# The ends of two hybrid layers, and their fifth unit: the splits of the third and fourth layer in another order on ScalarE and VectorE

## The chip, the cores and the metric

The kernel runs on one core of one Trainium2 chip. The metric is the device time in microseconds. Engine names are those of the profile: PE is TensorE, DVE is VectorE, ACT is ScalarE, POOL is GpSimd, SP is SyncE, which here issues every DMA.

## What is computed

Four layers run one after another on a stream x of 512 positions by 1024 channels, in float32. The first two (a gated spatial and pooling mixer, and latent attention with 16 heads) are not touched. The last two are one and the same hybrid layer with different weights:

```
def hybrid_layer(x, c_act, norm_g, w_ada, b_ada, w_in, w_out, pos):
    shift, scale, gate = jnp.split(c_act @ w_ada + b_ada, 3, axis=-1)
    h = rms_norm_2(x, norm_g) * (1.0 + scale[:, None, :]) + shift[:, None, :]
    rq, rk, rv, rg, sq, sk, sv, sg = jnp.split(h @ w_in, split_at, axis=-1)
    y_ret = retention(rotary(rq), rotary(rk), rv)        # 4 heads of 128
    y_ret = merge_heads(y_ret) * jax.nn.silu(rg)
    y_sb = stick_breaking(sq, sk, sv)                    # 8 heads of 64
    y_sb = merge_heads(y_sb) * jax.nn.silu(sg)
    y = jnp.concatenate([y_ret, y_sb], axis=-1) @ w_out
    return x + gate[:, None, :] * y
```

Retention multiplies the scores of each head by a decay, multiplies them with the values, and normalises the result over the 128 channels of the head. Stick-breaking attention takes sigmoids of the scores and a running product over the keys.

## The kernel before

Every large matmul is done in three passes on values that are split in a high and a low part: `mm3` issues high times low (L832 to L834 in some order of operands), low times high and high times high. The high part is a rounding copy (ACT or POOL), the low part is the difference of the value and its high part (DVE). Weights come in tiles of 128 by 2048 through two buffers that alternate (and some spare ones). For each tile T, SP transfers `w_raw` once the low part of tile T-2 is done (L797), ACT writes `w_hi` (`split_tile`, L1341), DVE writes `w_lo` (L1622). SP also transfers one piece of the modulation weights with each tile, `ada_raw` (L804), behind a wait that the piece two before it has been summed by DVE (`ada_piece`, L1655 and L1663).

All engines walk the same list, `plan_steps`, and each does its own part of every step, in the list's order. So the list is the order of the queue of each engine. An operation "tile" stands at the start of each tile T: PE waits for the low part of T; ACT makes the high part of T+1, DVE its low part, and then DVE sums the ada piece that goes with T, unless the step says `late_ada`.

A hybrid layer has eight units, u = 0 to 7. Units 0 to 3 are pairs of stick-breaking heads (`SP_PAIRS` is 4), units 4 to 7 retention heads. Each has five chunks of projection: AQ and AK (first tile), AV and AG (second tile), and VT, which turns the values over. AQ, AK, AV and AG are 24 matmuls of 512 columns each. The attention of the unit before (a = u-1) is put between them: `att_scores` ahead of AQ, `att_mid` behind AV, `att_out` behind AG (only for stick-breaking pairs: it ends in the two writes of `mixf` at L2170 and L2171). For a retention unit `att_scores` is 12 matmuls on PE, then on DVE four products with the decay (L2150), on ACT three high parts (L1591), on DVE three low parts (L2156); `att_mid` is 12 matmuls on PE and a square on ACT (L1611); then come `stat_cols` (column sums on PE L1201, a mean on DVE L1848, a root on ACT L1447, a reciprocal on DVE), `stat_bcast` (four transposes, L1210) and `ret_norm` (L2178, L2179), which writes `mixf`. `att_scores` of unit 4 waits on PE until `mixf` of unit 3 is written.

The chunks AQ, AK and VT have work behind them ("post"). For a retention unit ACT copies the bank to `tmp` (L1417), DVE applies the rotation to AQ and AK (L1670 to L1674), POOL makes the high part (L2202), DVE the low part (L1788, or L1791 for VT). A bank takes its next chunk once the one before is copied out.

`mix_split` makes the high part (ACT, L1598, into `h_hi`) and the low part (DVE, L2185, into `h_lo`) of the mixed heads, in the order of MIX_ORDER, whose places 0 to 3 are the stick-breaking units and 4 to 7 the retention units 4 to 7. The output projection then starts with `out_part(i)`: six matmuls for place i into the banks of the first two output chunks, spread among the attention of the last unit. After them each output chunk is 24 matmuls, and DVE adds it to x (L1768). The end of a layer, from VT of the last unit on, reads in the list: six places of `mix_split`, VT, `stat_cols` of unit 6, `att_scores` of unit 7, `out_part` 0 to 3, `stat_bcast` and `ret_norm` of unit 6, `mix_split` of place 6, the tile step of the first output tile (with the split of the second), `att_mid` of unit 7, `out_part(4)`, `stat_cols`, `out_part(5)`, `stat_bcast`, `ret_norm`, `out_part(6)`, `mix_split` of place 7 with the ada piece on DVE, a `redux` (16 small matmuls, L968), `out_part(7)`, and the output chunks.

Of the kernel before, what the change touches and what calls it, by code (L numbers as in the profile page):

```python
# [40 lines left out]
SP_PAIRS = 4  # L41
# [3 lines left out]
SEC = 8  # L45
# [34 lines left out]
def plan_steps():  # L80

    steps = []
# [3 lines left out]
    redux_chunk = {}  # L86
    spare_tiles = []

    def begin(late_ada=False):

        T = st["T"]
        st["T"] += 1
        steps.append(dict(op="tile", T=T, late_ada=late_ada))
        return T

    def chunk(kind, T, tmp=True, post=True, cast=False, val=False, **kw):
# [88 lines left out]
    T = begin()  # L185
# [41 lines left out]
    for l in (2, 3):  # L227
# [11 lines left out]
        for u in range(8):  # L239
            a = u - 1  # L240
            T = begin()
            if u == 0:
                spare_tiles.append(begin())
            if a >= 0:
                steps.append(dict(op="att_scores", l=l, u=a, g=base + a))
            for sub, kind in enumerate(("AQ", "AK")):
                chunk(kind, T, l=l, u=u, g=base + u, sub=sub, tmp=u >= SP_PAIRS, cast=u >= SP_PAIRS,
                      val=u >= SP_PAIRS)
                if sub == 0 and 0 <= a < SP_PAIRS:
                    steps.append(dict(op="att_scores2", l=l, u=a, g=base + a))  # L250
                if sub == (u < SP_PAIRS) and 0 <= a < SP_PAIRS:
                    steps.append(dict(op="att_scores3", l=l, u=a, g=base + a))
                if sub == 0 and norm:
                    steps.append(dict(op="stat_bcast", **norm))
                    steps.append(dict(op="ret_norm", l=l, u=a - 1, s=norm["stat"]))
                    norm = None
            after_tile(T)
            T = begin() if u > 0 else spare_tiles[-1]
            chunk("AV", T, l=l, u=u, g=base + u, sub=0, tmp=False, post=False)
            if a >= 0:  # L260
                steps.append(dict(op="att_mid", l=l, u=a, g=base + a))
            chunk("AG", T, l=l, u=u, g=base + u, sub=1, tmp=False, post=False)
            if a >= 0:
                steps.append(dict(op="att_out", l=l, u=a, g=base + a))
            if u == 7:
                steps.append(dict(op="mix_split", l=l, part=range(6)))
            chunk("VT", None, l=l, u=u, g=base + u, tmp=u >= SP_PAIRS, cast=u >= SP_PAIRS)
            after_tile(T)
            if a >= SP_PAIRS:
                norm = stat(P, 1, False, "ret2", 7, (7,))  # L270

        out_tile = st["T"]
        C = st["C"] + 1

        def out_part(*part):
            steps.append(dict(op="out_part", l=l, T=out_tile, C=C, part=part))

        steps.append(dict(op="att_scores", l=l, u=7, g=base + 7))
        out_part(0, 1, 2, 3)
        steps.append(dict(op="stat_bcast", **norm))  # L280
        steps.append(dict(op="ret_norm", l=l, u=6, s=norm["stat"]))
        steps.append(dict(op="mix_split", l=l, part=(6,)))
        T = begin(late_ada=True)
        steps.append(dict(op="att_mid", l=l, u=7, g=base + 7))
        out_part(4)
        norm = stat(P, 1, False, "ret2", 7, (7,))
# [1 line left out]
        steps.append(dict(op="stat_bcast", **norm))  # L288
        steps.append(dict(op="ret_norm", l=l, u=7, s=norm["stat"]))
        out_part(6)  # L290
        steps.append(dict(op="mix_split", l=l, part=(7,)))
        redux((8, 9) if l == 2 else (11,), aside=True)
        out_part(7)
        for i in range(4):
# [11 lines left out]
def build(nc, wt, adat, colst, matst, rmatst, xt, pos, wst, bst, poolt, decayt, rot, out):  # L306
# [11 lines left out]
    with ExitStack() as ctx:  # L318
# [1008 lines left out]
        def _(act):  # L1327
# [102 lines left out]
            for d in steps:  # L1430
# [161 lines left out]
                elif op == "mix_split":  # L1592
                    l = d["l"]
                    act.wait_ge(chunk_full, AG_CHUNK[8 * (l - 2) + 7] + 1)
                    for i in d["part"]:
                        k = MIX_ORDER[i]
                        act.wait_ge(mixf_done, 8 * (l - 2) + i + 1)
                        act.activation(h_hi[:, k, :], mixf[:, k, :], ACT.Copy).then_inc(m_hi_done, 1)  # L1598
# [16 lines left out]
        def _(dve):  # L1615
# [341 lines left out]
            for d in steps:  # L1957
                op = d["op"]
                if op == "tile":
                    T = d["T"]  # L1960
                    for t in split_with(T):
                        split_tile(t)
                    if not d["late_ada"]:
                        ada_piece(T + 2 * SEC)
                elif op == "chunk":
                    if d["kind"] == "XB" and d["n"] == 0:
# [4 lines left out]
                            dve.memset(padded[:, i, 0:PAD], 0.0).then_inc(pad_done, 1)  # L1971
                        dve.wait_ge(pad_done, 4)
                    chunk(d)
                elif op == "spatial_rows":
                    dve.wait_ge(rows_full, 1)
                    for i in range(DC):
# [202 lines left out]
                    dve.tensor_tensor(mixf[:, k, :], mixf[:, k, :], bank[:, 7, :], ALU.mult).then_inc(mixf_done, 1)  # L2179
                elif op == "mix_split":  # L2180
                    l = d["l"]
                    for i in d["part"]:
                        k = MIX_ORDER[i]
                        dve.wait_ge(m_hi_done, DC * (l - 2) + i + 1)
                        dve.tensor_tensor(h_lo[:, k, :], mixf[:, k, :], f(h_hi[:, k, :]),  # L2185
                                          ALU.subtract).then_inc(m_lo_done, 1)
                    if d["part"] == (7,):
                        ada_piece(T + 2 * SEC)
                elif op == "final":
                    dve.wait_ge(stb_done, d["s"] + 1)  # L2190
                    for n in range(DC):
                        dve.scalar_tensor_tensor(outf[:, n, :], x[:, n, :], col("final_g", n), bank[:, 6, :],  # L2192
                                                 ALU.mult, ALU.mult).then_inc(fin_done, 1)
# [219 lines left out]
```

## Time and profile before

| | |
|---|---|
| median of three runs | 1371.79 us (1371.42 to 1375.32) |
| the profiled execution, its own time | 1372.84 us |
| its span, first to last instruction | 1371.0 us |
| mean granted clock of TensorE | 0.991 |
| PE busy | 1330.3 us, 97% of the span |
| DVE, ACT, POOL busy | 67%, 41%, 22% |

The third layer runs in this execution from about 790 us to 1062 us and the fourth from there to 1360 us; the fifth unit of the third layer lies around 900 us to 921 us, its end from 1003 us to 1027 us, and the fourth layer has the same at 1200 us and from 1303 us. PE matmuls are pipelined: a 512-column matmul is shown with some 0.4 us, and the next one starts some 0.23 us after it. So a stall of PE is read from the distance between starts, and from the idle time in brackets at the end of a row, with what released it.

### The profile page before, as it was taken

How to read it: one execution, taken by the hardware profiler on the slowest of the kernel's cores; microseconds unless marked ns; L12 is line 12 of the kernel's file. 1: busy time of each engine (PE TensorE's matmuls, PEld its weight loads, DVE VectorE, ACT ScalarE, POOL GpSimd, SP SyncE). 2: the span in 40 equal slices, each digit the busy share in tenths (PEclk: the TensorE clock that was granted, in tenths of full speed). 3: DMA queues.
4: the chain of work that ended last, by engine and by line, in shares of the span. 5: the costliest groups of instructions: out<-in, count | busy, mean ns of one | idle time of the engine just before them, and what ended most of it. 6: DMA issues, size and time to landing. Idle time of an engine off the chain costs nothing. (4 is left out here: it accounts for less than half of the span.)

```text
span 1371.0 us, 17377 instructions
## 1 busy us (share of the span) xinstructions
PE 1330.3 (97%) x6761; PEld 1124.6 (82%) x6761; DVE 912.7 (67%) x1325; ACT 563.5 (41%) x851; POOL 302.5 (22%) x204
## 2 busy tenths in 40 slices
PE   6999999999999999999999999999999999999997
PEld 5998888778888878888888788878878888888875
DVE  6754534774585578988578877776675577675553
ACT  2423222321254255666322566643441565633330
POOL 0200200054420015464344100011115200011123
PEclk9999999999999999999999999999999999999998
DMA  9644443323324421222434352222314222111211
GB/s 378 187 160 138 138 146 142 128 101 136 140 107 137 138 76 39 70 59 70 115 125 129 106 171 93 93 93 105 126 58 169 97 95 86 66 62 62 68 56 62
DMA packets 31379, 155.14 MB, mean 113 GB/s; under 512 B 4161, under 2 KB 4289, under 8 KB 20033
## 3 DMA queue, kind: packets, MB, share of 16 engines
q1 hardware_dynamic: 31296, 154.03, 33.3%
q8 instruction: 54, 0.88, 0.3%
q14 instruction: 29, 0.23, 0.1%
HBM read 151.92 MB, written 2.10 MB: 112 GB/s over the span
## 5 line engine op out<-in xcount | busy, mean ns | idle before, releaser
L832 PE MATMUL bank<-h_lo,w_hi 128*128 128x512 f32 x1008 | 397.3, 394 | 3.3 <-issue 1.3
L834 PE MATMUL bank<-h_hi,w_hi 128*128 128x512 f32 x1008 | 392.7, 390 | 0.0
L833 PE MATMUL bank<-h_hi,w_lo 128*128 128x512 f32 x1008 | 392.4, 389 | 0.0
L1622 DVE TENSOR_TENSOR w_lo<-w_raw,w_hi 128x2048 fp32r<-128x2048 f32 (+2 forms) x91 | 206.7, 2272 | 88.8 <-ACT w_hi L1341 88.7
L832 PEld LDWEIGHTS bank<-h_lo,w_hi 128*128 128x128 f32 x1008 | 189.3, 188 | 43.4 <-issue 5.5
L834 PEld LDWEIGHTS bank<-h_hi,w_hi 128*128 128x128 f32 x1008 | 189.2, 188 | 39.9
L833 PEld LDWEIGHTS bank<-h_hi,w_lo 128*128 128x128 f32 x1008 | 189.4, 188 | 38.1 <-issue 0.5
L1341 ACT ACTIVATE w_hi<-w_raw 128x2048 fp32r<-128x2048 f32 (+2 forms) x91 | 166.7, 1832 | 86.4 <-PE bank L834 78.2
L1417 ACT ACTIVATE tmp<-bank 128x512 f32<-128x512 f32 x48 | 28.6, 596 | 131.1 <-PE bank L834 120.0
L2202 POOL TENSOR_SCALAR q_dup<-rot_y 128x512 fp32r<-128x512 f32 x8 | 11.9, 1492 | 308.4 <-DVE rot_y L1674 308.4
L1663 DVE SCALAR_TENSOR_TENSOR acc<-ada_raw,cond_pair,acc 128x1024 f32<-128x1024 f32 x45 | 58.5, 1300 | 0.0
L832 PE MATMUL bank<-mixc_lo,w_hi 128*128 128x512 f32 x128 | 50.6, 396 | 0.0
L834 PE MATMUL bank<-mixc_hi,w_hi 128*128 128x512 f32 x128 | 49.9, 390 | 0.0
L833 PE MATMUL bank<-mixc_hi,w_lo 128*128 128x512 f32 x128 | 49.8, 389 | 0.0
L2119 DVE TENSOR_TENSOR_SCAN keep<-keep 128x127 f32<-128x127 f32 (+2 forms) x64 | 49.0, 807 | 0.4
L2215 POOL TENSOR_TENSOR sum<-sum,sqr 128x512 f32<-128x512 f32 x24 | 48.0, 2000 | 1.9
L1758 DVE SCALAR_TENSOR_TENSOR x<-bank,gate,x 128x512 f32<-128x512 f32 x16 | 12.0, 751 | 50.5 <-PE bank L834 50.4
L2293 POOL TENSOR_TENSOR rope_t<-qr_f,sin 32x512 f32<-32x512 f32 x28 | 37.9, 1352 | 33.2 <-ACT qr_f L1556 30.7
L2214 POOL TENSOR_TENSOR sqr<-x 128x512 f32<-128x512 f32 x24 | 36.6, 1525 | 24.7 <-DVE x L1768 23.6
L1663 DVE SCALAR_TENSOR_TENSOR acc<-ada_raw,cond,acc 128x1024 f32<-128x1024 f32 x28 | 41.0, 1464 | 0.0
L2202 POOL TENSOR_SCALAR mixc_hi<-sz 128x512 fp32r<-128x512 f32 x16 | 23.9, 1493 | 76.0 <-DVE sz L1908 76.0
L2202 POOL TENSOR_SCALAR mixa_hi<-park 128x512 fp32r<-128x512 f32 x8 | 11.9, 1492 | 124.9 <-DVE park L1731 124.9
(349 smaller groups left out, 2677.4 us busy)
## 6 DMA issues: line engine op xcount, KB each, us to landing
w_raw<-wt SPq DMA_DIRECT2D x83, 1024.0 KB, 6.1
ada_raw<-adat SPq DMA_DIRECT2D x96, 256.0 KB, 3.9
ada_raw<-adat SPq DMA_DIRECT2D x32, 512.0 KB, 3.6
ada_first<-adat SPq DMA_DIRECT2D x16, 512.0 KB, 12.2
w_raw<-wt SPq DMA_DIRECT2D x8, 640.0 KB, 5.2
spare_raw<-wt SPq DMA_DIRECT2D x3, 1024.0 KB, 5.7
x<-xt SPq DMA_DIRECT2D x4, 512.0 KB, 15.5
out<-outf SPq DMA_DIRECT2D x8, 256.0 KB, 2.2
```

What stands on the lines that cost most here:

```text
L832: pe.matmul(dst, ah, bl, start=start, stop=False, skip_group_check=True)
L833: pe.matmul(dst, al, bh, start=False, stop=False, skip_group_check=True)
L834: return pe.matmul(dst, ah, bh, start=False, stop=stop, skip_group_check=True)
L1341: act.activation(w_hi[wb[T]][:, 0:n], w_raw[wb[T]][:, 0:n], ACT.Copy).then_inc(w_hi_done, 1)
L1417: act.activation(dst, src, func, scale=scale, bias=bias).then_inc(chunk_taken, 1)
L1622: dve.tensor_tensor(w_lo[wb[T]][:, 0:n], w_raw[wb[T]][:, 0:n], f(w_hi[wb[T]][:, 0:n]), ALU.subtract).then_inc(w_lo_done, 1)
L1663: dve.scalar_tensor_tensor(acc[:, g % 2, :], src, c, acc[:, g % 2, :], ALU.mult, ALU.add).then_inc(ada_done, 1)
L2119: ins = dve.tensor_tensor_scan(k, k, k, 1.0, ALU.mult, ALU.min)
L2202: return pool.tensor_scalar(dst, src, 1.0, None, ALU.mult)
L2214: link(pool.tensor_tensor(sqr[:], x[:, n, :], x[:, n, :], ALU.mult))
L2215: ins = pool.tensor_tensor(sum2[:], sum2[:], sqr[:], ALU.add)
L2293: pool.tensor_tensor(rope_t[to, :], qr_f[of, :], sin1[of, :], ALU.mult).then_inc(qr_turned, 1)
```

## The change

In the list of steps three things are altered, each for both hybrid layers.

The fifth unit (u = 4): on its second tile DVE makes the low part of the next weight tile and sums the ada piece behind `att_mid` of unit 3, no longer ahead of chunk AV. PE and ACT keep their order. For u = 5, `att_scores` of unit 4 stands between AQ and AK, no longer ahead of AQ, on all engines.

The end of a layer, first part: of the six places of `mix_split`, ACT makes the high parts of two ahead of VT and of four behind it. DVE makes the low parts of four ahead of VT's post and of two behind it.

The end of a layer, second part: the tile step of the first output tile stands right behind `att_scores` of unit 7, so ACT splits the second output tile there. DVE makes its low part behind `ret_norm` of unit 6, ahead of the low part of place 6. The ada piece on DVE that stood with `mix_split` of place 7 comes behind the post of the second output chunk (it exists in the third layer only; the pieces end before the fourth).

```
-            if a >= 0:
+            if a >= 0 and a != SP_PAIRS:
                 steps.append(dict(op="att_scores", l=l, u=a, g=base + a))
...
+                if sub == 0 and a == SP_PAIRS:
+                    steps.append(dict(op="att_scores", l=l, u=a, g=base + a))
...
-            T = begin() if u > 0 else spare_tiles[-1]
+            T = begin(late_ada=u == SP_PAIRS, late_low=u == SP_PAIRS) if u > 0 else spare_tiles[-1]
             chunk("AV", T, l=l, u=u, g=base + u, sub=0, tmp=False, post=False)
             if a >= 0:
                 steps.append(dict(op="att_mid", l=l, u=a, g=base + a))
+            if u == SP_PAIRS:
+                steps.append(dict(op="late_low", T=T, ada=True))
             chunk("AG", T, l=l, u=u, g=base + u, sub=1, tmp=False, post=False)
...
-                steps.append(dict(op="mix_split", l=l, part=range(6)))
+                steps.append(dict(op="mix_split", l=l, high=range(2), low=range(4)))
             chunk("VT", None, l=l, u=u, g=base + u, tmp=u >= SP_PAIRS, cast=u >= SP_PAIRS)
             after_tile(T)
+            if u == 7:
+                steps.append(dict(op="mix_split", l=l, high=range(2, 6), low=range(4, 6)))
...
         steps.append(dict(op="att_scores", l=l, u=7, g=base + 7))
+        T = begin(late_ada=True, late_low=True)
         out_part(0, 1, 2, 3)
         steps.append(dict(op="stat_bcast", **norm))
         steps.append(dict(op="ret_norm", l=l, u=6, s=norm["stat"]))
-        steps.append(dict(op="mix_split", l=l, part=(6,)))
-        T = begin(late_ada=True)
+        steps.append(dict(op="late_low", T=T, ada=False))
+        steps.append(dict(op="mix_split", l=l, high=(6,), low=(6,)))
         steps.append(dict(op="att_mid", l=l, u=7, g=base + 7))
...
-        steps.append(dict(op="mix_split", l=l, part=(7,)))
+        steps.append(dict(op="mix_split", l=l, high=(7,), low=(7,)))
...
                     chunk(d)
+                    if d["kind"] in ("OUT2", "OUT3") and d["n"] == 1:
+                        ada_piece(d["T"] + 2 * SEC)
...
-                    if d["part"] == (7,):
-                        ada_piece(T + 2 * SEC)
+                elif op == "late_low":
+                    for t in split_with(d["T"]):
+                        split_tile(t)
+                    if d["ada"]:
+                        ada_piece(d["T"] + 2 * SEC)
```

## Rows read from the trace of the kernel before

**Rows 1.** The page, part 1: busy time, share of the span, instructions.

```profile
PE 1330.3 (97%) x6761; PEld 1124.6 (82%) x6761; DVE 912.7 (67%) x1325; ACT 563.5 (41%) x851; POOL 302.5 (22%) x204
```

**Rows 2.** Waits of PE, 880 us to the end: total us, times, longest.

```profile
PE bank L832 <- issue: 3.5, 6, 0.7
PE bank L1201 <- ACT ret_sq L1611: 1.5, 2, 0.7
PE bank L832 <- DVE sp_lo L2163: 1.4, 1, 1.4
...
PE bank L832 <- DVE x L1768: 0.8, 2, 0.6
```

**Rows 3.** Timeline of PE, fifth unit of the third layer: start, duration.

```profile
908.91 0.48 PE L832 MATMUL bank<-h_lo,w_hi 128*128 128x512 f32 x1
...
916.02 0.47 PE L832 MATMUL bank<-sp_lo,av_hi 128*128 128x512 f32 x1 [1.41 <-DVE sp_lo L2163]
...
919.95 1.05 PE L1001 MATMUL bank<-mats,v_raw 128*128 128x128 f32 x8
921.64 0.47 PE L832 MATMUL bank<-q_dup,k_both 128*128 128x512 f32 x1 [0.64 <-issue]
...
923.58 0.45 PE L832 MATMUL bank<-h_lo,w_hi 128*128 128x512 f32 x1
```

**Rows 4.** Timeline of DVE there.

```profile
911.80 2.28 DVE L1622 TENSOR_TENSOR w_lo<-w_raw,w_hi 128x2048 fp32r<-128x2048 f32 x1
914.00 1.28 DVE L1663 SCALAR_TENSOR_TENSOR acc<-ada_raw,cond_pair,acc 128x1024 f32<-128x1024 f32 x1
915.20 3.08 DVE L2163 TENSOR_TENSOR sp_lo<-bank,sp_hi 128x512 fp32r<-128x512 f32 x5
...
920.84 0.69 DVE L2171 TENSOR_TENSOR mixf<-bank,ag 64x512 f32<-64x512 f32 x1
```

**Rows 5.** Timeline of PE, end of the third layer.

```profile
1003.15 1.05 PE L1001 MATMUL bank<-mats,v_raw 128*128 128x128 f32 x8
1004.04 0.95 PE L1201 MATMUL bank<-mats,ret_sq 128*128 128x1 f32 x8
1004.85 0.49 PE L832 MATMUL bank<-q_dup,k_both 128*128 128x512 f32 x1
...
1007.65 0.47 PE L832 MATMUL bank<-h_lo,w_hi 128*128 128x512 f32 x1 [0.67 <-issue]
...
1014.22 0.47 PE L832 MATMUL bank<-sp_lo,av_hi 128*128 128x512 f32 x1 [0.43 <-issue]
...
1018.50 1.05 PE L1201 MATMUL bank<-mats,ret_sq 128*128 128x1 f32 x8 [0.75 <-ACT ret_sq L1611]
...
1020.96 0.65 PE L1210 MATMUL bank<-mats,st_r 128*128 128x128 f32 x4
...
1024.56 0.50 PE L832 MATMUL bank<-h_lo,w_hi 128*128 128x512 f32 x1
...
1026.78 0.47 PE L832 MATMUL bank<-h_lo,w_hi 128*128 128x512 f32 x1 [0.55 <-DVE x L1768]
```

**Rows 6.** Timeline of ACT there.

```profile
1003.84 3.22 ACT L1598 ACTIVATE h_hi<-mixf 128x512 fp32r<-128x512 f32 x6
...
1016.07 1.90 ACT L1341 ACTIVATE w_hi<-w_raw 128x2048 fp32r<-128x2048 f32 x1
```

**Rows 7.** Timeline of DVE there.

```profile
1004.50 3.70 DVE L2185 TENSOR_TENSOR h_lo<-mixf,h_hi 128x512 fp32r<-128x512 f32 x6 [1.24 <-ACT h_hi L1598]
```

**Rows 8.** Timeline of POOL there.

```profile
1007.63 1.92 POOL L2202 TENSOR_SCALAR av_hi<-tmp 128x512 fp32r<-128x512 f32 x1 [8.50 <-ACT tmp L1417]
```

**Rows 9.** POOL's line L2202, 885 to 1060 us: ns, min, median, max.

```profile
L2202 POOL TENSOR_SCALAR av_hi<-tmp x4: 1492/1492/1924, 921.7 to 1007.6; 128x512 fp32r<-128x512 f32 x4
```

**Rows 10.** The page, part 6: DMA issues, KB each, us to landing.

```profile
w_raw<-wt SPq DMA_DIRECT2D x83, 1024.0 KB, 6.1
```

**Rows 11.** Busy time by stage between the hybrid layers; PEclk third from the end.

```profile
1064.00:1068.00 4.00, 4.00 (x12) 3.19 (x12) 1.94 (x7) 1.34 (x3) 0.95 (x2) 0.50 0.00 0
```

More of the change, by code:

```diff
@@ L87, in plan_steps, with begin @@
     spare_tiles = []
-    def begin(late_ada=False):
+    def begin(late_ada=False, late_low=False):
         T = st["T"]
         st["T"] += 1
-        steps.append(dict(op="tile", T=T, late_ada=late_ada))
+        steps.append(dict(op="tile", T=T, late_ada=late_ada, late_low=late_low))
         return T
@@ L265, in plan_steps @@
             if u == 7:
-                steps.append(dict(op="mix_split", l=l, part=range(6)))
+                steps.append(dict(op="mix_split", l=l, high=range(2), low=range(4)))
             chunk("VT", None, l=l, u=u, g=base + u, tmp=u >= SP_PAIRS, cast=u >= SP_PAIRS)
             after_tile(T)
+            if u == 7:
+                steps.append(dict(op="mix_split", l=l, high=range(2, 6), low=range(4, 6)))
             if a >= SP_PAIRS:
                 norm = stat(P, 1, False, "ret2", 7, (7,))
-        out_tile = st["T"]
         C = st["C"] + 1
         def out_part(*part):
-            steps.append(dict(op="out_part", l=l, T=out_tile, C=C, part=part))
+            steps.append(dict(op="out_part", l=l, T=T, C=C, part=part))
         steps.append(dict(op="att_scores", l=l, u=7, g=base + 7))
+        T = begin(late_ada=True, late_low=True)
         out_part(0, 1, 2, 3)
@@ L1594, in _ @@
                     act.wait_ge(chunk_full, AG_CHUNK[8 * (l - 2) + 7] + 1)
-                    for i in d["part"]:
+                    for i in d["high"]:
                         k = MIX_ORDER[i]
@@ L1960, in _ @@
                     T = d["T"]
-                    for t in split_with(T):
-                        split_tile(t)
+                    if not d["late_low"]:
+                        for t in split_with(T):
+                            split_tile(t)
                     if not d["late_ada"]:
@@ L2181, in _ @@
                     l = d["l"]
-                    for i in d["part"]:
+                    for i in d["low"]:
                         k = MIX_ORDER[i]
@@ L2186, in _ @@
                                           ALU.subtract).then_inc(m_lo_done, 1)
-                    if d["part"] == (7,):
-                        ada_piece(T + 2 * SEC)
+                elif op == "late_low":
+                    for t in split_with(d["T"]):
+                        split_tile(t)
+                    if d["ada"]:
+                        ada_piece(d["T"] + 2 * SEC)
                 elif op == "final":
```

## The prediction

> **What bounds the kernel now.** I read the page's busy times first: PE is busy for 97% of the span [rows 1]. So only time in which PE stands still, or runs slower, can be won; work moved between ACT and DVE is worth nothing by itself. Then the waits of PE in the two hybrid layers [rows 2]: 1.4 us once for `sp_lo`, six waits put down to "issue" with 3.5 us together, 1.5 us in two for `ret_sq`, 0.8 us in two for x. The timeline places them. In the fifth unit of the third layer `att_out` of unit 3 waits 1.41 us and `att_scores` of unit 4 waits 0.64 us [rows 3]. At the layer's end `out_part(0)` waits 0.67, `att_mid` of unit 7 waits 0.43, `stat_cols` 0.75 and the third output chunk 0.55 us [rows 5]. The six "issue" waits are 0.64, 0.67 and 0.43 twice (3.48), so the fourth layer has these three as well, and the same 0.75 for `ret_sq`; the wait for x is there 0.8 less 0.55, some 0.24 us, and `sp_lo` is not waited for.
>
> The step of PE: at 916.02 the matmul before ended 1.41 us earlier and had started 0.39 us before that, at 914.22; from 908.91 that is 23 steps of 0.231 us [rows 3]. I take 0.23 for a 512-column matmul (1.4 us for the six of an `out_part`), and 1.94 us for the twelve of unit 4's scores, to the start of the next chunk (921.64 to 923.58) [rows 3]; `att_mid` has the same shapes.
>
> **Fifth unit, low part and ada piece behind `att_mid`.** Before, DVE does the low weights from 911.80, the ada piece from 914.00, and only at 915.20 the five `sp_lo` [rows 4]. AG is out of PE at 914.22 + 0.23 = 914.45, `att_out` starts at 916.02. With the order turned, the five start at 911.9, take 3.08 us, the first is there 0.6 us later and the last at 915.0, ahead of its use. The stall goes: 916.02 - 914.45 = 1.57 us, and 0.1 us of slow first steps behind it, say **1.65 us**, in the third layer alone. What is late instead: the low weights are done at 917.3 and the piece at 918.5. The low weights are needed by AQ of u = 5, which PE reaches at about 919.2, so 1.9 us are left. `mixf` of unit 3 needs DVE at about 918.5, just free. SP's next weight transfer stands behind the ada wait and is issued 3.2 us later; it takes 6.1 us [rows 10] and is used one whole tile later, some 17 us on.
>
> **`att_scores` of unit 4 behind AQ.** It waits for the last `mixf` write, which starts at 920.84 and takes 0.69 [rows 4]; PE starts 0.1 us behind that. VT to the next work takes 1004.04 - 1003.15 = 0.89 us where nothing waits [rows 5], here 921.64 - 919.95 = 1.69 [rows 3]. AQ needs no `mixf`, and its 24 steps (5.5 us) cover the wait: **0.80 us** in each layer. Behind it on DVE: AQ's rotation, POOL's high part (which waits for the scores, then long out), AQ's low part, then the decay products. The low scores are ready some 3.5 us ahead of `att_mid`, and AK's post 6 us ahead of unit 5's scores. If the cover failed, the 0.80 would come back.
>
> **The layer's end, the first gap.** ACT makes six high parts from 1003.84, in 3.22 us, and only then, at 1007.0, copies VT out of the bank that `out_part(0)` needs [rows 6]; that is the 0.67. PE could have been there at 1004.85 + 1.94 = 1006.79 [rows 5], so 0.86 us are to be had. With two high parts ahead the copy starts at 1004.9 and ends at 1005.5, well in time. So PE does `out_part` 0 to 3 from 1006.79 and then wants `att_mid` of unit 7 at about 1012.65. This hangs on DVE, behind whose queue the low scores of unit 7 end. From the end of POOL's cast of VT at 1009.55 [rows 8] to `att_mid` at 1014.22 [rows 5] are 4.67 us on DVE and ACT: VT's low part, the mean, the root, the four products, three high and three low parts. In the new order two of the six low parts, 0.62 each (3.70 / 6) [rows 7], move between VT's low part and the mean.
>
> When does the cast end? It can start at 1005.5. Low parts 0 and 1 are done by 1005.7; numbers 2 and 3 have to wait for their high parts, from 1006.0 on. The one slow cast in the trace, 1.92 us, is the one that started while the low parts ran [rows 8]; three others took 1.49 [rows 9]. 1009.55 less 1.49 is 1008.06, about where the six low parts end (1004.50 + 3.70) [rows 7]. So a low part keeps the cast off. I take it to hold the other way too: cast from 1005.6 to 1007.1, then low parts 2 and 3, VT's low part, low parts 4 and 5, the rest. That is 1007.1 + 4 x 0.62 + 4.67 = 1014.25. `att_mid` comes where it came before, and **the 0.86 us are given back**. If the cast and the low parts run beside each other, two of the four are hidden (1.2 us): 1013.0, and 1.2 us won, which is the bound on the good side.
>
> The Trainium skill, SBUF — State Buffer, "SBUF: two separate sides", says that DVE and GpSimd share a port pair, that an instruction holds it whole, and that a DVE instruction with two SBUF inputs is one that takes it; whichever comes first, the other blocks. The trace agrees for the one direction it shows. By that rule the sum is the one I use; without it each layer would gain 1.2 us more.
>
> **The layer's end, from `att_mid` on.** Before: 1014.22 to 1024.56, 10.34 us [rows 5]. ACT's weight split from 1016.07, 1.90 us [rows 6], holds up the square, and PE's column sums start at 1018.50. Now the split stands ahead of it: the last high score must be out one low part (0.62 us) ahead of `att_mid`, so by 1013.6; ACT splits until 1015.5 at the latest, makes high part 6 until 1016.2, and is free as the square becomes due. Free of waits PE takes 1.94 (`att_mid`), 1.4 (`out_part(4)`), 0.81 (column sums, 1004.04 to 1004.85), 1.4 (`out_part(5)`), and then as before 3.60 (1020.96 to 1024.56, in which `ret_norm`, high and low part of place 7 just keep up with PE, so nothing is to be had there). Sum 9.1: **1.25 us** in each layer. DVE: `ret_norm` to 1015.5, the moved low weights (2.28, [rows 4]) to 1017.8, low part 6 to 1018.4, the mean at once; the reciprocal is out at 1019.2 and PE asks for it at 1019.7. The slack is 0.5 us: if the split is later than that, each further us is one of PE's.
>
> **The ada piece behind the second output chunk.** It took 1.28 us on DVE right ahead of the first x update. The third layer's wait for x becomes the fourth's: 0.55 - 0.24 = **0.3 us**. The piece now ends some 2 us into the third output chunk, and SP's next weights are issued then; with 6.1 us [rows 10] they land 8.5 us into the 11 us after which ACT splits them. Were they late, DVE's low part would come later, itself one tile ahead of its use; PE sees nothing below 5 us.
>
> **The sum.** 1.65 + 2 x 0.80 + 2 x (0 + 1.25) + 0.3 = 6.05 us, say 6.1. From the profiled execution's 1372.84: 1366.7. The median of the runs is 1.05 us lower, 1371.79, so I predict **1365.7 us**, 0.44% less. The gain of 0.3%, about what a measurement of this kernel can tell from no change, is 4.1 us.
>
> **The rivals.**
> *Cast and low parts run side by side.* For it: no row shows a low part kept waiting by a cast. Against it: the same two engines, and the slow cast. 2 x 1.2 us more: 1363.3 us. Chance 0.22.
> *The tail keeps its length.* The moved split and low weights meet the chain `ret_norm`, low part 6, mean, root: 0.5 us of slack. Place: `stat_bcast` of unit 7. At 1.7 us late nothing of the 1.25 is left: 2.5 us less saved, 1368.2 us. Chance 0.12.
> *Slower: TensorE's clock.* Between the hybrid layers the granted clock is at 0.50 for 4 us, the 1.2 GHz level, where PE has small matmuls [rows 11]; mostly it waits there anyway. At that level a 512-column step takes up to twice 0.23 us. If such stretches fell into dense matmuls, each 6 us of them would cost 3 us; the kernel is no faster from 12 us and slower by 0.3% from 20 us of them (6.1 + 4.1 over 0.5), 1376 us. Against it: the change takes stalls away and adds none. Chance 0.03. A stretch that only shifts against the layers' border moves the time by 2 us either way; that is in the range.
> *The fifth unit gives nothing*, because another step on DVE is late there: 3.2 us less, 1368.9 us. Chance 0.05.
>
> The forecast has 0.58. Its own range is 1364 to 1367.5. The range of all, 8 in 10, goes from the first rival to the second: **1362.8 to 1368.6 us**. Faster by over 0.3% (under 1367.7): the forecast and the first rival nearly whole, 0.85 with a little of the others; within 0.3%: 0.12; slower: 0.03.
>
> **What would show it.** No wait of PE for `sp_lo` in the third layer; AQ straight behind VT in the fifth unit, with scores 5.5 us later; `out_part(0)` 1.94 us behind the scores; a longer wait than 0.43 ahead of `att_mid` of unit 7, about 1.5 us, with POOL's cast at 1.5 us and DVE's low parts behind it (0.4 or less would be the first rival); no wait for `ret_sq`; 9.1 us from `att_mid` to `out_part(7)`; 0.24 us for x. The prediction is wrong if a new wait stands at `stat_bcast` of unit 7, or if the clock at the borders costs other than before.

## Result, and the profile after

The changed kernel takes **1363.39 us** in the median of four runs (1362.48 to 1366.07), beside 1371.96 us of four runs of the kernel before. The ratio is 0.9932, with a 95% interval of 0.9914 to 0.995: faster by 0.7%. The forecast was 1365.7 us, 0.44%. The profiled execution took 1363.42 us, its span is 1361.6 us. PE is still the bound. Its busy time, on the page's first lines, fell by 2.8 us against [rows 1]; the other 6.6 us of the shorter span are time in which it stood still.

```profile
PE 1327.5 (97%) x6761; PEld 1123.4 (83%) x6761; DVE 912.9 (67%) x1325; ACT 563.5 (41%) x851; POOL 303.3 (22%) x204
```

The waits of PE from 880 us to the end (total, times, longest), which answer to [rows 2]:

```profile
PE bank L1216 <- DVE st_r L1856: 0.8, 1, 0.8
PE bank L1195 <- ACT sqr L1451: 0.7, 1, 0.7
PE bank L838 <- DVE x L1774: 0.5, 2, 0.2
PE bank L1276 <- issue: 0.4, 1, 0.4
PE bank L838 <- DVE sp_lo L2165: 0.4, 1, 0.4
```

The six "issue" waits at the 512-column matmuls, the two for `ret_sq` and the 1.4 for `sp_lo` of unit 3 are gone. The 0.8 for `st_r` and the 0.7 for `sqr` lie at the border between the hybrid layers and at the end and were there before. The 0.4 for "issue" at L1276 was there before too. New is 0.4 for `sp_lo` of L2165: that is `att_mid` of unit 7, in the fourth layer.

The timeline of PE, fifth unit and end of the third layer, against [rows 3, 5], and one row of the fourth:

```profile
908.44 0.48 PE L838 MATMUL bank<-h_lo,w_hi 128*128 128x512 f32 x1
...
913.99 0.39 PE L838 MATMUL bank<-sp_lo,av_hi 128*128 128x512 f32 x1
...
917.81 1.05 PE L1007 MATMUL bank<-mats,v_raw 128*128 128x128 f32 x8
918.62 0.47 PE L838 MATMUL bank<-h_lo,w_hi 128*128 128x512 f32 x1
...
924.18 0.39 PE L838 MATMUL bank<-q_dup,k_both 128*128 128x512 f32 x1
...
1001.05 0.95 PE L1207 MATMUL bank<-mats,ret_sq 128*128 128x1 f32 x8
1001.86 0.49 PE L838 MATMUL bank<-q_dup,k_both 128*128 128x512 f32 x1
...
1003.83 0.45 PE L838 MATMUL bank<-h_lo,w_hi 128*128 128x512 f32 x1
...
1009.35 0.60 PE L1216 MATMUL bank<-mats,st_r 128*128 128x128 f32 x4
1010.01 0.50 PE L838 MATMUL bank<-sp_lo,av_hi 128*128 128x512 f32 x1
...
1013.41 0.95 PE L1207 MATMUL bank<-mats,ret_sq 128*128 128x1 f32 x8
...
1019.25 0.50 PE L838 MATMUL bank<-h_lo,w_hi 128*128 128x512 f32 x1
...
1021.14 0.47 PE L838 MATMUL bank<-h_lo,w_hi 128*128 128x512 f32 x1 [0.24 <-DVE x L1774]
...
1305.00 0.50 PE L838 MATMUL bank<-sp_lo,av_hi 128*128 128x512 f32 x1 [0.38 <-DVE sp_lo L2165]
```

`att_out` of unit 3 starts 5.55 us behind AG (7.11 before), AQ 0.81 behind VT's transposes, `out_part(0)` 1.97 behind the scores, and `att_mid` of unit 7 comes 8.15 us behind the scores (9.37 before). Cut at such starts, the two executions compare stage by stage. Every number is a distance between two starts on PE, third / fourth layer:

| stage | before | after | saved |
|---|---|---|---|
| fifth unit, AG to VT | 11.04 / 9.37 | 9.37 / 9.36 | 1.67 / 0 |
| VT to `att_mid` of unit 4 | 20.03 / 20.03 | 19.18 / 19.18 | 0.85 / 0.85 |
| column sums of unit 6 to `out_part(0)` | 3.61 / 3.61 | 2.78 / 2.78 | 0.83 / 0.83 |
| `out_part(0)` to `att_mid` of unit 7 | 6.57 / 6.57 | 6.18 / 6.50 | 0.39 / 0.07 |
| `att_mid` to `out_part(7)` | 10.34 / 10.35 | 9.24 / 9.23 | 1.10 / 1.12 |
| `out_part(7)` to the third output chunk | 2.22 / 1.90 | 1.89 / 1.89 | 0.33 / 0 |

The saved column adds to **8.04 us**, where 6.05 were forecast. The spans differ by 9.4. The remaining 1.36 lie in three stretches that the change does not touch: 0.47 ahead of the third layer's fifth unit, 1.39 from the third layer's output chunks to the fourth's fifth unit (183.37 before, 181.98 after), and 0.5 the other way at the end. Whether these belong to the change is asked below.

Now the place the forecast turned on. DVE, POOL and ACT at the end of the third layer, against [rows 6 to 8]:

```profile
1001.50 1.29 DVE L2194 TENSOR_TENSOR h_lo<-mixf,h_hi 128x512 fp32r<-128x512 f32 x2 [1.25 <-ACT h_hi L1604]
1003.03 1.39 DVE L2194 TENSOR_TENSOR h_lo<-mixf,h_hi 128x512 fp32r<-128x512 f32 x2 [0.23 <-ACT h_hi L1604]
1004.34 0.68 DVE L1797 TENSOR_TENSOR av_lo<-tmp,av_hi 128x512 fp32r<-128x512 f32 x1
1004.94 1.28 DVE L2194 TENSOR_TENSOR h_lo<-mixf,h_hi 128x512 fp32r<-128x512 f32 x2
1006.14 0.15 DVE L1854 TENSOR_SCALAR st_var<-bank 128x4 f32<-128x4 f32 x1
```

```profile
1002.56 1.59 POOL L2214 TENSOR_SCALAR av_hi<-tmp 128x512 fp32r<-128x512 f32 x1 [6.43 <-ACT tmp L1423]
```

```profile
1001.89 0.59 ACT L1423 ACTIVATE tmp<-bank 128x512 f32<-128x512 f32 x1
1002.37 2.19 ACT L1604 ACTIVATE h_hi<-mixf 128x512 fp32r<-128x512 f32 x4
...
1008.97 1.90 ACT L1347 ACTIVATE w_hi<-w_raw 128x2048 fp32r<-128x2048 f32 x1
...
1012.18 0.60 ACT L1617 ACTIVATE ret_sq<-bank 128x512 f32<-128x512 f32 x1
```

The forecast had low parts 2 and 3 start when the cast ends. They start at 1003.03, 1.12 us before its end at 1004.15, waiting only for their high parts. VT's low part follows at 1004.34, 0.19 us behind the cast and not 1.24.

### The profile page after: what moved, and what is told of

It is laid out like the page before. It is cut to its first block, busy times and chain, and to the rows that moved or that the text cites. A ratio compares the mean times of both kernels' runs of the same rounds, so it can differ in the third digit from the quotient of the medians.

```text
span 1361.6 us, 17379 instructions
## 1 busy us (share of the span) xinstructions
PE 1327.5 (97%) x6761; PEld 1123.4 (83%) x6761; DVE 912.9 (67%) x1325; ACT 563.5 (41%) x851; POOL 303.3 (22%) x204
## 4 chain that ended last, share of the span: by engine, by line
PE 87%; DVE 6%; issue 3%; ACT 3%; DMA 1%; SPq 0%; POOL 0%; DVEq 0%; ACTq 0%; POOLq 0%
PE bank L838 25%; PE bank L840 24%; PE bank L839 24%; PE bank L845 1%; PE bank L1302 1%; PE bank L992 1%; PE bank L1136 1%; PE bank L1276 1%; DVE acc L1669 1%; PE bank L1278 1%; PE bank L974 1%; DMA ada_first<-adat 1%; PE bank L1123 1%; PE bank L1140 1%; DVE qn_lo L1928 1%
```

## Experiments

### Each part by itself

Four kernels, each the kernel before with one part of the change. They ask whether the parts add, and which part owns which stage. The ratio of every experiment is against runs of the kernel before that were made beside it, so medians are compared only among kernels that share them (e1 to e4; e5 to e7, with 1373.73 us for the kernel before; the others with 1372.46); otherwise the stages are compared.

`e1_low_only`: low part and ada piece of the fifth unit behind `att_mid`.

```diff
-            T = begin() if u > 0 else spare_tiles[-1]
+            T = begin(late_ada=u == SP_PAIRS, late_low=u == SP_PAIRS) if u > 0 else spare_tiles[-1]
...
+            if u == SP_PAIRS:
+                steps.append(dict(op="late_low", T=T, ada=True))
```

> The kernel before with one part of the change: in the fifth unit DVE makes the next low weights and sums the ada piece behind att_mid. Forecast's sum: the 1.41 us wait for sp_lo in the third layer goes, att_out starts 1.57 us earlier against AG, 1.65 us in all, nothing in the fourth layer: 1370.1 us. Rival (parts are not additive, the low weights are late for AQ of the sixth unit without the moved scores): a new wait ahead of the scores or of AQ of u = 5, under 1 us gained.

`e2_scores_only`: `att_scores` of unit 4 between AQ and AK.

```diff
-            if a >= 0:
+            if a >= 0 and a != SP_PAIRS:
                 steps.append(dict(op="att_scores", l=l, u=a, g=base + a))
...
+                if sub == 0 and a == SP_PAIRS:
+                    steps.append(dict(op="att_scores", l=l, u=a, g=base + a))
```

> The kernel before with one part: att_scores of unit 4 between AQ and AK. Forecast's sum: AQ starts 0.89 us behind VT instead of 1.69 us later, 0.80 us in each layer, 1.6 us: 1370.2 us; the 1.41 us wait for sp_lo stays. Rival: a rotation that waits on POOL, which waits for the scores, makes DVE late, and PE waits at att_mid of unit 4; then 0 to 0.8 us are gained.

`e3_split_only`: high and low parts split around VT, the output tile's step where it was.

```diff
-                steps.append(dict(op="mix_split", l=l, part=range(6)))
+                steps.append(dict(op="mix_split", l=l, high=range(2), low=range(4)))
...
+            if u == 7:
+                steps.append(dict(op="mix_split", l=l, high=range(2, 6), low=range(4, 6)))
```

> The kernel before with one part: high parts two ahead of VT and four behind, low parts four ahead of VT's post and two behind. Theory A (the low parts run beside POOL's cast): out_part(0) 0.86 us earlier and att_mid of unit 7 1.2 us earlier in each layer, 2.4 us: 1369.4 us, with the 0.75 us wait for ret_sq still there. Theory B, as forecast (the cast holds the low parts off): out_part(0) 0.86 us earlier, att_mid where it was, 0 us: 1371.8 us. Theory C (the gain in the changed kernel needs the moved tile step): under 0.5 us.

`e4_tile_only`: the output tile's step behind the last scores, its low part behind `ret_norm` of unit 6, the six places in one block as before.

```diff
+        T = begin(late_ada=True, late_low=True)
         out_part(0, 1, 2, 3)
...
-        T = begin(late_ada=True)
+        steps.append(dict(op="late_low", T=T, ada=False))
```

> The kernel before with one part: the first output tile's step behind the last scores, low weights ahead of the low part of place 6, and the ada piece behind the second output chunk. Forecast's sum: att_mid of unit 7 where it was; column sums and the rest 1.1 to 1.25 us earlier in each layer, 0.3 us for x in the third: 2.5 to 2.8 us: 1369.1 us. Rival (the chain of the mean has only 0.5 us of slack and without the other part meets it): a wait at stat_bcast of unit 7, 1.5 us gained or less.

Measured against the kernel before (1372.59 us in 31 runs, these in ten each); the stages are third / fourth layer:

| kernel | median | ratio | saved by stages |
|---|---|---|---|
| `e1_low_only` | 1371.67 | 0.9991 [0.9981, 1.0001] | 1.66 / 0, AG to VT |
| `e2_scores_only` | 1370.91 | 0.9989 [0.9979, 1.0] | 0.86 / 0.85, VT to `att_mid` of unit 4 |
| `e3_split_only` | 1370.52 | 0.9982 [0.9972, 0.9992] | 1.06 / 0.88, layer's end |
| `e4_tile_only` | 1369.72 | 0.9985 [0.9976, 0.9994] | 1.18 / 1.17, layer's end |

The medians are too near each other to rank the parts, and by its interval e1 can't be told from no change at all; the stages do rank them, and agree with the table above to 0.02 us for e1 and e2. The parts add: 1.66 + 1.71 + 1.94 + 2.35 = 7.66, and with the ada piece's 0.33 it is 8.0. That piece was left at place 7 in e4, against what its expectation says, so its 0.3 for x did not appear there (2.22 from `out_part(7)` to the third output chunk, as before); none of the four has it alone.

In e3 `att_mid` of unit 7 comes 1.18 / 0.87 us earlier behind the column sums, without the tile's step moved. So the first gap's time stays won by the split itself, as theory A has it; the median, 1370.52, lies between A's 1369.4 and B's 1371.8 and decides nothing. The timeline of PE in e3 has one row that explains why the third layer's end, with 1.18 us won there, saves only 1.06:

```profile
1018.82 1.05 PE L1203 MATMUL bank<-mats,ret_sq 128*128 128x1 f32 x8 [0.87 <-ACT ret_sq L1613]
```

`att_mid` has come nearer to the weight split on ACT, which was left in its old place, and the wait for the square is 0.87 us where it was 0.75 [rows 5].

### Do the low parts run beside the cast?

Two theories of the same trace. A: DVE's low parts run beside POOL's cast, so two of them are hidden in it. The other is the prediction's: the cast holds them off, and `att_mid` came early for some other reason. Each kernel changes how many low parts DVE has in its queue beside the cast; ACT's order is the changed kernel's.

```diff
 # e5_four_beside
-                steps.append(dict(op="mix_split", l=l, high=range(2), low=range(4)))
+                steps.append(dict(op="mix_split", l=l, high=range(2), low=range(6)))
...
-                steps.append(dict(op="mix_split", l=l, high=range(2, 6), low=range(4, 6)))
+                steps.append(dict(op="mix_split", l=l, high=range(2, 6), low=()))
 # e6_two_behind
+                steps.append(dict(op="mix_split", l=l, high=range(2), low=range(2)))
...
+                steps.append(dict(op="mix_split", l=l, high=range(2, 6), low=range(2, 6)))
```

> The changed kernel with all six low parts ahead of VT's post on DVE (ACT as in the change, two high parts ahead of VT's copy and four behind), so that four low parts meet POOL's cast. Theory A (side by side): low parts 2 to 5 follow their high parts at 0.6 us each and end 1.2 to 1.4 us later than low part 3 did; VT's low part comes behind them; the mean 0 to 0.3 us earlier than in the changed kernel, att_mid as there or 0.2 us earlier, 1363 us. Theory B (the cast holds DVE): no low part between the cast's start and its end, the mean about 1 us later, att_mid too, 2 us more in all.

> The changed kernel with only low parts 0 and 1 ahead of VT's post and four behind it; nothing of DVE beside the cast. Theory A: the two low parts were hidden beside the cast, now they are not: the mean and att_mid of unit 7 come 1.2 us later in each layer, 2.4 us more: 1365.8 us. Theory B (the cast held them off anyway): no difference from the changed kernel, 1363.4 us.

e5: 1363.76 us, ratio 0.9933 [0.9915, 0.995]. Its DVE and POOL:

```profile
1004.79 2.59 DVE L2194 TENSOR_TENSOR h_lo<-mixf,h_hi 128x512 fp32r<-128x512 f32 x4 [0.23 <-ACT h_hi L1604]
1007.31 0.68 DVE L1797 TENSOR_TENSOR av_lo<-tmp,av_hi 128x512 fp32r<-128x512 f32 x1
```

```profile
1004.33 1.59 POOL L2214 TENSOR_SCALAR av_hi<-tmp 128x512 fp32r<-128x512 f32 x1 [6.42 <-ACT tmp L1423]
```

Four low parts go through in 2.59 us, the first from 0.46 us behind the cast's start. `out_part(0)` to `att_mid` is 6.19 / 6.19, in the third layer as in the changed kernel. e6: 1365.81 us, ratio 0.9947 [0.9929, 0.9964], with DVE idle from 1002.1 us until the cast ends at 1003.49:

```profile
1003.62 0.69 DVE L1797 TENSOR_TENSOR av_lo<-tmp,av_hi 128x512 fp32r<-128x512 f32 x1 [1.48 <-POOL av_hi L2214]
1004.23 2.49 DVE L2194 TENSOR_TENSOR h_lo<-mixf,h_hi 128x512 fp32r<-128x512 f32 x4
```

There the stage is 7.35 / 7.35: `att_mid` comes 1.17 / 0.85 us later. That is what two hidden low parts are worth. A holds, and it is the stages that show it. The medians of e5 and e6 differ by 2.05 us, but their intervals overlap, and that e6 came out at the 1365.8 expected is luck: the changed kernel itself gave 1363.39 in one group of runs and 1365.01 in another.

### What does hold a low part up?

A leaves two questions: why the cast ran beside the subtractions at all, and why it took 1.92 us in the kernel before [rows 8]. A1 says that it is the cast's single input: a POOL instruction with two inputs would hold DVE's subtraction. D1 says that a subtraction already under way delays the cast. e7 makes VT's high part as a product with ones; e10 puts the cast behind more high parts, so that it falls due while DVE is in the middle of its row of low parts.

```diff
 # e7_cast_two_in
-                            ins = cast(av_hi[:].rearrange("p b r -> p (b r)"), t)
+                            ins = pool.tensor_tensor(av_hi[:], t.rearrange("p (b r) -> p b r", b=NB),
+                                                     ones.rearrange("p (a r) -> p a r", a=1).broadcast_to([P, NB, P]), ALU.mult)
 # e10_cast_second
-                steps.append(dict(op="mix_split", l=l, high=range(2), low=range(4)))
+                steps.append(dict(op="mix_split", l=l, high=range(4), low=range(6)))
...
+                steps.append(dict(op="mix_split", l=l, high=range(4, 6), low=()))
```

> The changed kernel with POOL's cast of VT (retention units) written as a product with ones, two inputs from SBUF instead of one. The output is the same. Theory A1 (a POOL instruction with two inputs takes turns with a DVE instruction with two inputs, one with one input does not): low parts 2 and 3 beside it become longer or the cast does, 1 us and more together, att_mid 0.5 us later or more. Theory A2 (the number of inputs does not matter, only that DVE was not waiting): the low parts keep 1.39 us for two, and the cast takes what a product takes without DVE beside it, 1.0 us by the squares of the output chunks, or 1.5 as now; att_mid as in the changed kernel or up to 0.4 us earlier.

> The changed kernel with four high parts of ACT ahead of VT's copy and all six low parts ahead of VT's post on DVE, so that POOL's cast becomes due while DVE is in a run of low parts. Theory D1 (a DVE subtraction that runs holds the cast until it ends, and the next one runs beside it): the cast takes 1.5 to 2.1 us by the profile, the low parts keep 0.62 us each. Theory D2 (back to back subtractions keep the cast out as long as they last): the cast ends 1.5 us behind the last low part, 3 us by the profile, the mean and att_mid 1 us later. Theory D3 (the cast does not wait for DVE at all, and the 1.92 us of the kernel before have another cause): 1.5 to 1.6 us.

e7: 1365.38 us, ratio 0.9946 [0.9929, 0.9963]. POOL, in a place where DVE is idle and at the layer's end, and the low parts on DVE by tile (ns, min/median/max):

```profile
973.20 1.29 POOL L2250 TENSOR_TENSOR av_hi<-tmp,mats 128x512 fp32r<-128x512 f32 x1 [5.99 <-ACT tmp L1423]
...
1001.74 1.39 POOL L2250 TENSOR_TENSOR av_hi<-tmp,mats 128x512 fp32r<-128x512 f32 x1 [6.62 <-ACT tmp L1423]
```

```profile
L2194 DVE TENSOR_TENSOR h_lo<-mixf,h_hi x6: 677/682/1469, 1000.7 to 1005.4; 128x512 fp32r<-128x512 f32 x6
```

One low part, begun at 1002.21 in the middle of the product, lasts 1.47 us and ends 0.55 us behind the product's end at 1003.13. So it did almost nothing until then. The product is 0.10 us longer than where DVE is idle; the two together lose 0.9 us, a little under the 1 us expected. The product is 0.2 us shorter than the cast, and still `att_mid` is 0.70 / 0.37 us later (6.88 / 6.87). A1 is borne out, as far as this run goes: it doesn't part the second input from its repeated reading of one block, nor from the other operation. The trace of the kernel before has a row that does for the repeated block. There POOL adds two whole tensors (L2215, from 1050.87 to 1054.31 us), and a subtraction of 2048 columns begins under it:

```profile
1053.07 3.38 DVE L1622 TENSOR_TENSOR spare_lo<-spare_raw,spare_hi 128x2048 fp32r<-128x2048 f32 x1
```

It takes 3.38 where the one of [rows 4] took 2.28, and ends 2.15 us behind the sum's end. So a POOL instruction with two inputs holds the subtraction without any repeated reading. e10 (1365.3 us, ratio 0.9943 [0.9928, 0.9957]), POOL and then DVE by tile:

```profile
1007.93 1.76 POOL L2214 TENSOR_SCALAR av_hi<-tmp 128x512 fp32r<-128x512 f32 x1 [7.46 <-ACT tmp L1423]
```

```profile
L2194 DVE TENSOR_TENSOR h_lo<-mixf,h_hi x6: 679/686/954, 1005.8 to 1009.3; 128x512 fp32r<-128x512 f32 x6
```

The cast takes 1.76 instead of 1.49. A low part had begun at about 1007.7, so at the cast's start some 0.4 us of it were left. Three casts line up: 0.23 us left and 0.10 longer (the changed kernel), 0.4 left and 0.27 longer (e10), 0.57 left and 0.43 longer (before: the sixth low part ends at 1004.50 + 3.70, the cast starts at 1007.63 [rows 7, 8]). In each the cast is longer by what was left, less 0.13 or 0.14. The trace of the kernel before has the same in the first layer, with much more left:

```profile
276.57 3.46 POOL L2202 TENSOR_SCALAR mixb_hi<-park 128x512 fp32r<-128x512 f32 x1
```

A subtraction of 2048 columns ran there until 278.67, 2.11 us were left, and the cast is 1.97 longer than 1.49. That supports D1: the cast waits for the subtraction that is under way, and for no more. Of the subtractions one took 0.95 in e10, and the first behind the cast's start 0.78 in the changed kernel, in place of 0.69 (D1 had expected no loss): being beside a cast costs them a tenth to a quarter of a us once. The stage is 6.19 / 6.20, as in e5.

### The same kernel again

`a1_changed_again` is the changed kernel without an edit, to see how much of the 1.36 us outside the changed stages comes with the code.

> The changed kernel as it is, for direct comparison with the two kernels below on the same chip. By the stages of its first profile 8.05 us of the 9.4 us between the two profiled spans belong to the change, the rest to the starting DMA and to stretches at the lower clock; the median should be 8 us under the kernel before, give or take 1.5.

1365.01 us in five runs (1363.96 to 1367.04), ratio 0.9945 [0.9933, 0.9957]; the span of its profile is 1365.2. The changed stages are those of the table to 0.02 us. From the third layer's output chunks to the fourth's fifth unit it takes 183.35 us: the kernel before had 183.37, the changed one 181.98. The busy time of the border at 1045 to 1080 us, granted clock third from the end; first before, then after, then this run:

```profile
1045.00:1080.00 35.00, 35.00 (x159) 29.48 (x158) 21.95 (x30) 12.95 (x14) 18.73 (x14) 0.90 0.24 91
```

```profile
1045.00:1080.00 35.00, 35.00 (x166) 29.15 (x165) 24.09 (x30) 11.19 (x14) 15.67 (x12) 0.95 0.32 117
```

```profile
1045.00:1080.00 35.00, 35.00 (x159) 29.57 (x159) 24.86 (x31) 12.95 (x14) 16.56 (x12) 0.90 0.23 85
```

The granted clock of 0.90 against 0.95 goes with the 1.4 us, and the same code shows both. All 13 profiles of this document fall in three groups on the way from the third layer's output chunks to the fourth's fifth unit: 183.35 and 183.37 us where the border is at 0.90 (before, and this run), 181.80 to 182.49 in nine with 0.95, 180.87 and 181.44 in two with 1.00 (e9 and e8). Ahead of the third layer's fifth unit, too, the same code took 908.44 us once and 910.67 the other time. So the 1.36 us are no more than one kernel differs from itself. The 8.04 us of the stages are 0.59% of 1371.8, a ratio of 0.9941, which lies in the intervals of both measurements.

### What is left at the layer's end

Two waits stayed: 0.3 us ahead of `att_mid` of unit 7 (0.6 in the fourth layer), and 0.24 for x. `e8_two_after_scores` moves the last two low parts from behind VT's low part to behind the low scores of unit 7. `e9_and_other_bank` also gives the third output chunk another bank of PE's, so that it doesn't wait until the x update has read its own.

```diff
 # both
-                steps.append(dict(op="mix_split", l=l, high=range(2, 6), low=range(4, 6)))
+                steps.append(dict(op="mix_split", l=l, high=range(2, 6), low=()))
...
         steps.append(dict(op="att_scores", l=l, u=7, g=base + 7))
+        steps.append(dict(op="mix_split", l=l, high=(), low=range(4, 6)))
 # e9 alone
+            other = d is OUT0_FIRST or d["kind"] in ("OUT2", "OUT3") and d["n"] == 2
+            bk = CHUNK_BANK[d["C"]] = (2 + d.get("sub", 0)) if aside else 2 if other else d["C"] % 2
```

> The changed kernel with low parts 4 and 5 on DVE moved from ahead of the mean to behind the three low scores of unit 7. Theory (the chain cast, low parts, mean, scores is what att_mid waits for): the mean 1.2 us earlier, the wait ahead of att_mid gone, 0.25 us in the third layer and 0.55 in the fourth, 0.8 us less than the changed kernel; out_part(4) and ret_norm of unit 6 unhurt. Rival: ret_norm of unit 6, the moved low weights and the mean of unit 7 come 1 us later by the two low parts, and a wait of up to 0.7 us appears at stat_bcast of unit 7; then nothing is gained.

> As the one before, and the third output chunk of each hybrid layer goes into a bank of its own, so that it need not wait for the first update of x. Theory: the 0.24 us wait for x goes in both layers, with its slow first steps 0.3 us each, 0.6 us less than the kernel before it, 1.4 us less than the changed kernel. Rival: the wait turns up at the fourth or fifth chunk, 0 us.

e8: 1364.3 us, ratio 0.9942 [0.9927, 0.9958]; no difference from `a1_changed_again`. Its DVE:

```profile
1005.42 0.15 DVE L1855 TENSOR_SCALAR st_var<-bank 128x4 f32<-128x4 f32 x1
1006.68 0.18 DVE L1857 RECIPROCAL st_r<-st_sd 128x4 f32<-128x4 f32 x1 [1.11 <-ACT st_sd L1454]
...
1009.90 1.29 DVE L2195 TENSOR_TENSOR h_lo<-mixf,h_hi 128x512 fp32r<-128x512 f32 x2
```

`out_part(0)` to `att_mid` is 5.87 / 5.88, so that wait is gone (0.31 / 0.62), but less than the 1.2 us of the two moved low parts: the mean is out 1.2 earlier, and the reciprocal then waits 1.11 us for the root, since on ACT a table load, which stands behind the high parts, lasts from 1005.06 to 1006.34. And it is given back: the two low parts, at 1009.90, now stand ahead of `ret_norm` of unit 6, so ACT's high part 6 and with it the square come later, and from `att_mid` to `out_part(7)` it takes 9.54 / 9.52 where it took 9.24 / 9.23. Net 0 / 0.32 us.

e9: **1361.92 us** (1360.22 to 1364.93), ratio 0.9924 [0.9911, 0.9938], the fastest of all. Its waits of PE from 880 us on have no x any more:

```profile
PE bank L1218 <- DVE st_r L1858: 0.8, 1, 0.8
PE bank L1197 <- ACT sqr L1453: 0.7, 1, 0.7
PE bank L1278 <- issue: 0.4, 1, 0.4
PE bank L1006 <- ACT v_raw L1425: 0.3, 1, 0.3
PE bank L840 <- DVE h_lo L1807: 0.3, 1, 0.3
```

`out_part(7)` to the third output chunk takes 1.52 / 1.49 (0.38 / 0.42 less than in e8), and the time stays won to the last matmul of the output chunks, so the wait did not turn up at a later one. By the stages e9 is 1.1 us faster than the changed kernel. Its median is 3.1 us under that of `a1_changed_again`, with intervals that overlap; the rest above 1.1 is of the size that the clock moved between two profiles of one kernel. In e9's profile the border is at 1.00, and a part of its low time is that.

## Why the prediction was right and wrong

**The bound and the places were right.** Everything that the change won lies at a wait of PE that [rows 2, 3, 5] showed. The measured 1363.39 us is 2.3 under the forecast and below its own range of 1364 to 1367.5, and 0.1 from the 1363.3 of the rival of cast and low parts side by side. That closeness is luck in part: 1.36 of the 9.4 us between the spans are not the change's, and the same code gave 1365.01 in other runs.

**Fifth unit.** 1.65 forecast for the low part behind `att_mid`, 1.67 measured, in the third layer alone; `e1_low_only` has 1.66. 0.80 for each layer's scores, 0.85 measured; `e2_scores_only` has 0.86 / 0.85 (VT to AQ is 0.81 us, not 0.89). No other step became late there, so the rival that the unit gives nothing is out.

**The step that failed is the first gap of the layer's end.** It was put as "I take it to hold the other way too", and so "the 0.86 us are given back". The split won the first gap as forecast (0.83), but `att_mid` came 0.39 / 0.07 earlier behind `out_part(0)` instead of 0.86 later: together 1.22 / 0.90 us where the sum had 0. The rival had said 1.2 for each layer. It was the true case. The 2.12 us of this term explain the 2.0 that the stages lie above the sum, with 0.3 too much in the term of `att_mid` below, and 0.1 to 0.2 too little in those of the fifth unit and of x. e5 shows four low parts beside the cast at no loss, e6 what it costs when none are there, 1.17 / 0.85.

The working leant on one slow cast. That row showed only that a subtraction delays a cast which falls due under it; I turned it round without a row for it. And it was not "the one slow cast in the trace": [rows 9] stop at 885 and 1060 us, while the whole trace has seven, each begun under a DVE instruction with two inputs in SBUF. Nor is it true that "no row shows a low part kept waiting by a cast". The trace of the kernel before has rows of both in its second layer:

```profile
529.86 1.50 POOL L2202 TENSOR_SCALAR mixc_hi<-sz 128x512 fp32r<-128x512 f32 x1 [2.83 <-DVE sz L1908]
```

```profile
426.90 1.09 DVE L2090 TENSOR_TENSOR qc_lo<-qkv,qc_hi 128x512 fp32r<-128x512 f32 x1 [0.96 <-POOL qc_hi L2202]
530.64 0.68 DVE L1893 TENSOR_TENSOR rope_y<-rope_y,rope_t 128x512 f32<-128x512 f32 x1
```

The sum at 530.64, two inputs in SBUF, runs whole inside the cast of 529.86, and neither is longer for it; the subtraction at 426.90, 0.06 us behind the start of a cast of 1.49 us, is 0.4 us longer than the 0.69 of its like, and not by the whole cast. These rows stood against the forecast's case before anything was run. The Trainium skill, SBUF — State Buffer, "SBUF: two separate sides", says of the port pair that DVE and GpSimd share that whichever comes first holds it for its whole instruction and that the other blocks. Where the subtraction came first the runs agree (the casts of 1.76, 1.92 and 3.46 us). Where this cast with one input came first they don't: subtractions of two SBUF inputs ran beside it at 0.68 to 0.78 us each, 0.95 in e10. For the two-input product of e7 they do (1.47 us). The measurement decides: the rule, as I used it, was too wide.

**From `att_mid` on.** 1.25 forecast, 1.10 / 1.12 measured. The sum counted 1.94 + 1.4, 0.81 + 1.4 and 3.60, rounded down to 9.1; PE took 3.40, 2.29 and 3.55, so 9.24, with no wait in it. The term was large by 0.14 for each layer: 0.06 and 0.08 in the two parts with six matmuls at 1.4 us, 0.05 by the rounding of 9.15 to 9.1, less 0.05 of the 3.60. The slack of 0.5 held: the split on ACT ends at 1010.9, well ahead of high part 6 at 1011.49, and the rival that the tail keeps its length is out.

**The ada piece.** 0.3 forecast, 0.33 measured, third layer alone. That SP's next transfers went out later showed in no wait of PE.

**The clock.** It cost PE 1.4 us more or less at the border from one execution to another, both with the same code, which the range had taken in as 2 us either way. The rival of a slower clock did not come: the mean granted clock is 0.992 in the profile of the changed kernel and was 0.991.

**What stays open.** In the fourth layer of the changed kernel `att_mid` comes 0.32 us later than in the third, in both profiles and in e3, but not in e5 to e10. The timeline of DVE has the 0.22 us ahead of VT's low part, with both its inputs done (POOL's cast ended at 1298.82, the low part before it at 1299.09):

```profile
1297.70 1.39 DVE L2194 TENSOR_TENSOR h_lo<-mixf,h_hi 128x512 fp32r<-128x512 f32 x2 [0.23 <-ACT h_hi L1604]
1299.31 0.69 DVE L1797 TENSOR_TENSOR av_lo<-tmp,av_hi 128x512 fp32r<-128x512 f32 x1 [0.22 <-issue]
```

From the start of the low part before it to its own it is 0.90 us here and 0.60 in the third layer, so these 0.22 us and the overlap lost with them are the 0.3. What DVE does in them wasn't found.

## What to carry to other kernels

A lengthened instruction in a trace shows who waited for whom in one direction. Before a sum takes the other direction too, look for a row of it, in the whole trace and not only around the stage that is changed (here the second layer had it), and where there is none keep both ends as cases with their full size: here the one sentence was worth 2.1 of 8 us. When short instructions have to share the time of two engines, put the ones that need not wait beside the slow cast, and use the form of the cast that lets them pass, even where another form is shorter by itself (1.29 against 1.49 us, and 0.4 to 0.7 us slower in the end). And where medians of two variants lie closer than a kernel's own spread, compare distances between starts on the bounding engine in stages whose code is alike: they repeated to 0.02 us, while the spans of one kernel differed by 3.6.

## What the runs showed of the hardware

That POOL and DVE hold each other up differently in the two directions, and differently by the form of POOL's instruction. The cast of 128x512 to fp32r with one input took 1.49 us alone, and 1.59 in the changed kernel, in e5 and in e6, where two, four and no further subtractions ran beside it; the four took 2.59 us there and 2.49 alone (e6). The product with two inputs took 1.29 us alone and more than doubled the one subtraction that began under it. The other way round, a cast begun under a subtraction was longer by what was left of it, less some 0.14 us, from 0.23 us left to 2.11; under an instruction of DVE that reads one of its inputs from PE's bank (`qkv`, 425.38 us in the kernel before, 0.57 us left) it took its plain 1.49. Nor had I expected that the border between the hybrid layers takes 1.4 us more or less with the same code, which is more than any part of this change but the low part behind `att_mid` saves in a layer.
